# One load moved forward on SyncE's queue, and GpSimd's waits on the attention scores reduced to the first

## The reference

```python
kk = heads(k * k_k).astype(f32)
kk = kk / jnp.maximum(jnp.sqrt(jnp.sum(kk * kk, -1, keepdims=True)), 1e-12)
k_dir = heads(k[:, :, None, :] * (1.0 + (iclr - 1.0) * k_a))
y_fwd = wkv7_scan(rh, dec_h[:, :, 0], k_dir[:, :, 0], vh, -kk, kk * a_h[:, :, 0], True)
...
def attend(q_blk):
    s = jnp.einsum('bqhd,bkhd->bhqk', q_blk, k).astype(jnp.float32) * scale
    prob = jax.nn.softmax(s, axis=-1)
    return jnp.einsum('bhqk,bkhd->bqhd', prob.astype(v.dtype), v)
```

## Time and profile before

| | us |
|---|---|
| median of 3 runs | 1570.64 |
| lowest, highest | 1568.95, 1572.15 |
| the profiled execution, its own time | 1570.64 |
| its span in the profile | 1568.8 |
| PE busy | 1520.7 |
| DVE busy | 1043.6 |
| ACT busy | 636.4 |
| POOL busy | 345.8 |

### The profile page before, as it was taken

The page is one execution under the profiler, slowest core; times in us unless marked ns, Lnnn a source line. Parts: engine busy times, 40 slices in busy tenths (PEclk is TensorE's granted clock), DMA queues, the critical chain, the costliest instruction groups (busy, mean ns, idle before and its releaser), DMA issues.

```text
span 1568.8 us, 25838 instructions
## 1 busy us (share of the span) xinstructions
PE 1520.7 (97%) x10160; PEld 1101.0 (70%) x10160; DVE 1043.6 (67%) x1503; ACT 636.4 (41%) x1178; POOL 345.8 (22%) x356
## 2 busy tenths in 40 slices
PE   6999999999999999999999999999999999999998
PEld 5788775645555556777754467888888888888786
DVE  7424589778666576666557489775555555689877
ACT  6212246656444444444430225433333333334553
POOL 0900014123410038888810140220000000000000
PEclk9999999999999999999999999999999999999999
DMA  6131010010000010001041012332221211756322
GB/s 245 54 147 53 20 54 14 7 28 13 12 24 12 7 32 3 2 2 29 2 182 74 0 54 69 127 122 86 81 81 54 57 62 44 275 195 207 115 68 108
DMA packets 29001, 110.70 MB, mean 71 GB/s; under 512 B 3568, under 2 KB 6096, under 8 KB 26720
## 3 DMA queue, kind: packets, MB, share of 16 engines
q1 hardware_dynamic: 28432, 103.97, 19.4%
q0 software_dynamic: 464, 5.28, 0.8%
HBM read 89.36 MB, written 18.92 MB: 69 GB/s over the span
## 4 chain that ended last, share of the span: by engine, by line
PE 71%; issue 12%; DVE 9%; POOL 5%; ACT 2%; DMA 1%; DVEq 0%; SPq 0%; POOLq 0%; ACTq 0%
PE psum L2908 24%; PE psum L2925 12%; PE psum L2832 7%; PE psum L2578 4%; PE psum L2605 3%; PE psum L2496 2%; PE psum L2612 2%; PE psum L2515 1%; PE psum L2466 1%; POOL arena L852 1%; POOL arena L854 1%; PE psum L2806 1%; PE psum L2701 1%; PE psum L2719 1%; PE psum L2715 1%
## 5 line engine op out<-in xcount | busy, mean ns | idle before, releaser
L1987 DVE TENSOR_TENSOR part_lo<-arena,part_hi 128x512 fp32r<-128x512 f32 x154 | 117.8, 768 | 77.3 <-ACT part_hi L1268 77.1
L2908 PE MATMUL psum<-h_hi,part_hi 128*128 128x512 f32 x616 | 165.7, 391 | 1.1 <-ACT arena L1316 0.7
L2908 PE MATMUL psum<-h_lo,part_hi 128*128 128x512 f32 x616 | 164.7, 389 | 0.0
L2908 PE MATMUL psum<-h_hi,part_lo 128*128 128x512 f32 x616 | 164.6, 389 | 0.0
L1268 ACT ACTIVATE part_hi<-arena 128x512 fp32r<-128x512 f32 x154 | 95.9, 628 | 132.6 <-PE psum L2908 114.9
L2908 PEld LDWEIGHTS psum<-h_hi,part_hi 128*128 128x128 f32 x616 | 115.2, 188 | 26.7 <-ACT arena L1316 1.1
L2908 PEld LDWEIGHTS psum<-h_lo,part_hi 128*128 128x128 f32 x616 | 115.7, 188 | 24.1
L2908 PEld LDWEIGHTS psum<-h_hi,part_lo 128*128 128x128 f32 x616 | 115.7, 188 | 24.0
L918 POOL TENSOR_TENSOR arena<-arena,consts 128x512 f32<-128x512 f32 x64 | 81.9, 1300 | 135.2 <-ACT arena L1169 134.6
L2832 PE MATMUL psum<-arena 128*128 128x512 f32 x256 | 110.5, 592 | 0.0
L1657 DVE TENSOR_REDUCE stats<-psum 128x1 f32<-128x1024 f32 x64 | 77.8, 1216 | 44.9 <-PE psum L2496 44.7
(11 more groups left out here) (329 smaller groups left out, 3025.7 us busy)
## 6 DMA issues: line engine op xcount, KB each, us to landing
arena<-in_w_gate SPq DMA_DIRECT2D x22, 512.0 KB, 3.7
arena<-in_w_up SPq DMA_DIRECT2D x22, 512.0 KB, 3.7
arena<-in_w_down SPq DMA_DIRECT2D x22, 512.0 KB, 3.6
arena<-in_w_down SPq DMA_DIRECT2D x11, 1024.0 KB, 5.0
arena<-in_w_in SPq DMA_DIRECT2D x15, 512.0 KB, 3.5
arena<-act_spill SPq DMA_DIRECT2D x12, 512.0 KB, 7.0
act_spill<-arena SPq DMA_DIRECT2D x10, 512.0 KB, 6.0
arena<-in_x SPq DMA_DIRECT2D x8, 512.0 KB, 8.1
```

What stands on the lines that cost most here:

```text
L1987: v.tensor_tensor(lo, raw[:, at:at + HALF], hi, ALU.subtract).then_inc(part_lo, 1)
L2908: mm = pe.matmul(bank({2: z, 3: y, 5: y}.get(p, x)), w[:, P * k:P * k + P], h[k // 2][:, HALF * (k % 2):HALF * (k % 2) + HALF], start=(fre ...
```

## The change

On SP's queue the load of `ident` is issued behind the first tile of x, no longer behind the fourth. On POOL, the loop over q no longer waits for the scores of head q before its turn q: it waits once, ahead of the loop, for the first scores of head 0. The instructions themselves are the same, and the waits on `ex_ready` stay.

```diff
--- before.py
+++ after.py
@@ -643,7 +643,8 @@
         def _(sp):
             for t in range(4):
                 sp.dma_start(resid[:, t, :], a["x"][t]).then_inc(rows_in_place[t], 16)
-            sp.dma_start(ident, a["consts"][:, 0:P]).then_inc(ident_in, 16)
+                if t == 0:
+                    sp.dma_start(ident, a["consts"][:, 0:P]).then_inc(ident_in, 16)
             for s in range(NSLOT):
                 sp.dma_start(w_raw[s], a["w_in"][s]).then_inc(weights_in[s], 16)
             for t in range(4, NT):
@@ -892,9 +893,9 @@
             ones(1)
             pool.wait_ge(z_sig, 14)
             pool.wait_ge(kk_ready, 2)
+            pool.wait_ge(s_done, 1)
             for q in range(4):
                 hp = q % 2
-                pool.wait_ge(s_done, 8 * q + 1)
                 own.add(pool.tensor_tensor(Bt[:, q], Kt[:, q], kk[:, hp], ALU.mult))
                 own.wait()
                 own.add(pool.tensor_scalar(Kt[:, q], Kt[:, q], pcol("k_a", hp), one_less_ka[:, hp:hp + 1],
```

## The result

| | before | changed |
|---|---|---|
| median of 5 runs, us | 1571.60 | 1581.14 |
| lowest, highest | 1568.95, 1573.76 | 1578.62, 1582.40 |
| profiled execution: its own time, span | 1570.64, 1568.8 | 1581.29, 1579.4 |
| mean granted clock of PE in it | 0.999 | 0.995 |

The ratio is 1.0051 (95% interval 1.0039 to 1.0063): 9.5 us slower by the medians, 6.1 to 9.9 us by the interval. The forecast was 6.1 us slower and a range up to 1579.2 us: the direction was right, the time lies above the range. All 25 timed executions of the changed kernel have a median of 1579.66 us, so these five are on the slow side of it, and that median too is above the range.

A forecast was written before the change was run, and what follows sets the result against it. The prediction took PE, busy 97% of the span, to bound the kernel. Head 1's 6.0, head 2's -0.2 and the identity load's 0.3 gave +6.1 us on 1570.64: 1576.7 us, range 1571.2 to 1579.2.

The forecast's parts named there:

- The exclusion on POOL and DVE: In head 1, two-SBUF-input DVE instructions and POOL instructions exclude each other for their whole length: PE +6.0 us.
- the replay: Hand count of POOL's and DVE's timelines in heads 0 and 1 under the exclusion: head 0 +0, head 1 +6.0 us.
- rival A: Head 1: L1711 of q = 2 wins against POOL's L903; total +3.4 us, 1574.0 us; chance with its cousin 0.24.
- Rival B: Head 1: L1711 isn't held by POOL; total +1.5 us, 1572.1 us; chance 0.10.
- rival C: Head 1: DVE loses only slack, PE runs ahead by as much; +0.1 us, 1570.7 us; chance 0.16.
- Rival D: Head 1: L1709 is held too, L1711 waits for one more L898; up to +8.3 us, 1579.0 us; chance 0.08.
- over 4: Sign in head 1: the scan of q = 3 takes over 4 us instead of 2.28.
- the price of the identity load: At the start: x loads behind the identity load are issued 0.44 us later; between 0 and +0.44 us, +0.3 taken.
- the granted clock: PE's clock: no term for it in the forecast, no size given.
- -0.2: Head 2, free of POOL's work after the change: 0.20 us shorter.

The follow-up runs named there:

- e1: Kernel before with only the edit on POOL's waits, identity load where it was: 1576.58 us, +6.1 us, ratio 1.0038.
- e11: Changed kernel (both edits) with e7's order on DVE: 1577.60 us, +6.6 us against the kernel before, ratio 1.0035.
- e12: Kernel before with POOL's waits alone changed and e7's order on DVE: 1574.66 us, +3.7 us, ratio 1.0021.
- e7: Kernel before with DVE's two memsets, reciprocal and transpose moved behind head 0's first row maxima: 1568.09 us, -2.7 us, ratio 0.9983.
- e8: Changed kernel's POOL waits, identity load as before, POOL's products for q = 1, 2, 3 replaced by memsets: ran once, read by trace, L1642 1.22 us.
- e3: Kernel before with only POOL's q = 1 started at once behind q = 0: 1570.85 us, +0.3 us, ratio 0.9999.
- e4: Kernel before with only POOL's q = 2 moved, to follow q = 1 inside head 1: 1573.90 us, +3.4 us, ratio 1.0015.
- e2: Kernel before with only the identity load moved: 1572.20 us, +1.7 us, ratio 1.0009.

## Why the prediction was right in its mechanism and short in its size

**The exclusion on POOL and DVE** held step by step. L1711, whose being held was inferred from L1642 alone, is held (3.33 us), the times of the table agree with the replay to within 0.2 us, and the close race of L903 against L1711 (rival A) went as counted, in the changed kernel, e1, e11 and e12 alike. Head 1 grew by 6.2 us where 6.0 were forecast, and by itself the edit costs 6.1 us in e1 and 6.6 over e7 in e12. Rival B (L1711 isn't held) and rival C (slack takes it up) are refuted; e8 shows for the two-input instructions that POOL's reading is what matters, and e3 that the same collision behind q = 1 alone is free. DVE and POOL are thus ordered here by more than their semaphores. So the cost is the chain of q = 2 and q = 3 inside head 1: e4, q = 2 alone, has about half of it.

**Rival D was half right.** L1709 is held too, but it doesn't cost a further POOL instruction: it waits in L1711's stead (2.13 us at 389.83), and L1711 follows at 392.00, before POOL's next (0.05 us behind it), and takes 1.23 us. So L1711 of q = 3 ends where the replay had it, though the replay had the wait on L1711. The second scan took 3.26 us and not "over 4": it started 1 us later than replayed, since PE had gone to half clock at 382 us, but its end is set by the end of POOL's L908, as replayed (2.15 us behind it). In e8 POOL's writing alone seems to hold L1709, which the rule of the replay, of two-input instructions, doesn't cover.

**The step that failed: the price of the identity load.** "Between 0 and +0.44 us" took the delay of the later issue as the upper bound. Measured, PE's first transposes come 1.58 us later, and about as late in both other traces with the load there; e2 has +1.7 us in time, though its interval (0.0 to 2.8) doesn't exclude the forecast's 0.3 by itself. The bound was of the wrong kind: it priced the issue, and not when the next x tile lands. In the trace of the changed kernel this doesn't show at the first scores (POOL's first L898 is 0.26 us later only), since the projection loop of the profiled execution before ran 11.20 us a turn (e7's too) where the changed kernel's has 11.09 (the others 10.98 or 11.09), about 1.2 us in all. No run says why the turn differs, and the edits don't touch it.

**The term that was missing: the granted clock.** The prediction had PE at one clock all through, because its trace did. All four traces in which PE waits 2.44 us in head 1 (the changed kernel, e1, e11, e12) have 3 to 7 us at 1.2 GHz right behind it. In the changed kernel's trace this stretch is largely hidden behind ACT's wait of 1.49 us for L1711; another in head 2 makes that head 1.4 us longer (10.77 us behind at its end, 9.36 at its start), where the sum had -0.2; and the one in head 0 made that head 2.9 us longer. Over the runs the size isn't separable exactly: the changed kernel's 25 executions average a clock of 0.9958 where the kernel before averages 0.9969 to 0.9972 in its three groups, and within the changed kernel those at 0.997 take 1577.5 us and those at 0.995 1580.7. A mean lower by 0.0011 to 0.0014 is about 2 us of full clock over the whole execution, of which a part is hidden: so 1 to 2 us of the whole are put down to it, as an estimate.

The sum: 6.2 in head 1, 1.6 at the start, an estimated 1 to 2 for the clock, together 9 to 10, for a measured 9.5. How the excess over the forecast divides isn't shown by the times: the two edits apart give 7.8 us (6.1 and 1.7), the clock of their runs included, and both the 7.8 and the forecast's 6.1 still touch the interval of 6.1 to 9.9. Another 1.0 us of the missed time is none of the change's: the forecast was built on 1570.64, the median of three runs, and that of five is 1571.60. That the size came out above the range is so in part the draw of the runs; the two wrong terms are not. The change itself has no gain on the other side: POOL ended its loop 34 us earlier (401.67 us for 435.67) and nobody waited for it.

## What to carry to other kernels

Waits that look like needless caution on an engine off the critical path can be what keeps its work away from another engine's; before taking them out, list which instructions of the two exclude each other (here: DVE with two SBUF inputs, POOL reading SBUF) and replay both timelines at the new place, as was possible here to 0.2 us. Then add what can follow a stall of PE: look in several executions for stretches at a lower granted clock, since one trace may not have them. And close a stall of PE even where it seems small: moving 1.5 us of DVE work by one or two slots gave 2.7 us (interval 1.4 to 4.1).

## What had not been expected of the hardware

- A 64 KB load or a 512 KB load issued right behind the first x tile makes the second come 1.7 to 2.6 us later (7.57 to 8.43 us for 5.85 or earlier); the same 64 KB ahead of the first or behind the second tile made the next tile 0.2 to 0.6 us late.
- In PE's stall of 1.8 us in head 0 or within 2 us behind it, its clock went to 0.50 for 3 to 7 us in eight of the eleven traces that have this stall, and in head 0 of none of the three without it (e7, e11, e12).
- A DVE instruction on 128x8 elements with one SBUF input (L1709, a strided read) is held by POOL as well: 1.16 to 2.15 us for 0.16; in one row also by a memset, which reads nothing (0.38 us, e8).
